# Making the high and low activation parts of two expert slots in one operation each

## The reference

```python
u = jnp.take(expert_u, eidx, axis=0)
a = jnp.einsum('thkd,td->thk', u, hc).astype(jnp.float32)
act = (jax.nn.gelu(a, approximate=False) * g).astype(hc.dtype)
vv = jnp.take(expert_v, eidx, axis=0)
return jnp.einsum('thk,thkd->td', act, vv)
```

## Time and profile before

| what | value |
|---|---|
| runs | 1316.86, 1319.37, 1319.6 us (median 1319.37) |
| profiled execution | 1320.85 us, of which 1318.7 us span |
| TensorE (PE) busy | 1304.0 us, 99% of the span |
| PE weight loads (PEld) busy | 1258.2 us, 95% |
| VectorE (DVE) busy | 1015.2 us, 77% |
| ScalarE (ACT) busy | 827.2 us, 63% |
| GpSimd (POOL) busy | 525.0 us, 40% |
| granted TensorE clock, mean | 0.997 of full speed |
| second expert layer | 674 to 1001 us of the span |

### The profile page before, as it was taken

The page is one execution under the profiler, slowest core; times in us unless marked ns, Lnnn a source line. Parts: engine busy times, 40 slices in busy tenths (PEclk is TensorE's granted clock), DMA queues, the critical chain, the costliest instruction groups (busy, mean ns, idle before and its releaser), DMA issues.

```text
span 1318.7 us, 24814 instructions
## 1 busy us (share of the span) xinstructions
PE 1304.0 (99%) x9818; PEld 1258.2 (95%) x9818; DVE 1015.2 (77%) x1845; ACT 827.2 (63%) x1679; POOL 525.0 (40%) x252
## 2 busy tenths in 40 slices
PE   9999999999999999999999999999999999999998
PEld 8999899999999999999999899999999999999997
DVE  4483645859999888899978798998867845899943
ACT  5564646545456888888865565555566666666653
POOL 3745567678901000000024444424205463794442
PEclk9999999999999999999999999999999999999999
DMA  8434345555656555555479999998865544556552
GB/s 301 139 111 128 118 139 177 165 175 177 196 189 200 199 168 167 162 174 162 164 249 332 353 332 328 327 343 316 310 212 169 171 133 130 188 166 196 186 191 97
DMA packets 74298, 268.35 MB, mean 203 GB/s; under 512 B 8252, under 2 KB 8636, under 8 KB 74184
## 3 DMA queue, kind: packets, MB, share of 16 engines
q1 hardware_dynamic: 64392, 232.17, 52.9%
q0 software_dynamic: 9216, 33.56, 6.9%
q10 hardware_dynamic: 576, 1.05, 0.2%
HBM read 265.70 MB, written 1.05 MB: 202 GB/s over the span
## 4 chain that ended last, share of the span: by engine, by line
PE 86%; DVE 10%; ACT 1%; DMA 1%; issue 0%; POOL 0%; SPq 0%; DVEq 0%; ACTq 0%
PE PS L611 85%; DMA RAW<-in_ev 1%; ACT SPL L1096 1%; DVE HS L1578 1%; DVE ixu L1839 1%; DVE Ssc L1833 1%; DVE ixu L1830 1%; PE PS L754 1%; DVE SPL L1549 1%; DVE bias L1628 0%; DVE top L1836 0%; DVE top L1827 0%; DVE HF L1566 0%; DVE qpc L1879 0%; DVE abu L1895 0%
## 5 line engine op out<-in xcount | busy, mean ns | idle before, releaser
L1096 ACT ACTIVATE SPL<-RAW 128x1024 fp32r<-128x1024 f32 x429 | 453.7, 1059 | 366.1 <-PE PS L611 350.7
L611 PE MATMUL PS<-HS,SPL 128*128 128x224 f32 (+2 forms) x3968 | 531.2, 292 | 1.1 <-DVE SPL L1549 0.9
L611 PEld LDWEIGHTS PS<-HS,SPL 128*128 128x128 f32 x3968 | 502.4, 189 | 12.7 <-issue 1.7
L2268 POOL TENSOR_TENSOR SPL<-RAW,SPL 128x1024 fp32r<-128x1024 f32 x149 | 361.7, 2432 | 261.1 <-ACT SPL L1096 261.1
L1549 DVE TENSOR_TENSOR SPL<-RAW,SPL 128x1024 fp32r<-128x1024 f32 x280 | 345.1, 1234 | 143.5 <-ACT SPL L1096 141.2
L611 PE MATMUL PS<-asp,SPL 128*128 128x448 f32 (+1 forms) x2048 | 321.9, 319 | 3.2 <-DVE SPL L1549 1.9
L611 PEld LDWEIGHTS PS<-asp,SPL 128*128 128x128 f32 x2048 | 307.5, 190 | 17.2 <-DVE SPL L1549 2.1
L2298 POOL DMA_INDIRECT rows<-in_er,RS x16 | 28.2, 1763 | 278.3 <-PE PS L611 247.7
L611 PE MATMUL PS<-HXb,SPL 128*128 128x256 f32 x720 | 89.3, 284 | 0.8 <-issue 0.6
L611 PEld LDWEIGHTS PS<-HXb,SPL 128*128 128x128 f32 x720 | 87.4, 188 | 1.4 <-issue 1.1
L1312 ACT ACTIVATE oh<-oh,T3f 128x128 f32<-128x128 f32 x224 | 71.4, 404 | 0.0
(11 more groups left out here) (296 smaller groups left out, 1529.5 us busy)
## 6 DMA issues: line engine op xcount, KB each, us to landing
RAW<-in_dense SPq DMA_DIRECT2D x176, 512.0 KB
RAW<-in_eu SPq DMA_DIRECT2D x128, 512.0 KB
RAW<-in_ev SPq DMA_DIRECT2D x128, 512.0 KB
bias<-in_nab SPq DMA_DIRECT2D x2, 768.0 KB, 6.9
XT<-in_xT ACTq DMA_DIRECT2D x4, 256.0 KB, 7.1
out_y<-HF SPq DMA_DIRECT2D x4, 256.0 KB, 2.2
c<-in_c SPq DMA_DIRECT2D x1, 960.0 KB, 9.0
c<-in_c SPq DMA_DIRECT2D x1, 512.0 KB, 4.7
```

The costliest lines, as they stand in the source:

```text
L611: return e.matmul(out, l, r, start=start, stop=stop, skip_group_check=skip)
L1096: e.activation(spl(n)[0], raw(n), ACT.Copy).then_inc(*up("act_high", ("hi", n)))
L2268: e.tensor_tensor(lo, raw(n), hi.bitcast(f32), ALU.subtract).then_inc(*up("pool_low", ("lo", n)))
```

## The change

The "a" steps 4 to 127 become 62 steps "a2", each for two neighbouring slots. Step "a2" of activations i and i + 1 stands before v step j = i - 2, for even j from 2 to 124. ScalarE writes both high parts in one operation (448 values per partition, into two regions of `asp`), after waiting for TensorE to be done with slot i - 3. VectorE makes both low parts in one operation, and both keys "apart" are given by that one. Activations 0 to 3 are made one by one as before. A region of the pair i, i + 1 was last used by slots i - 4 and i - 3.

```diff
@@ peer_steps
     for j in range(NE):
-        while ahead < min(j + 4, NE):
-            yield "a", ahead
-            ahead += 1
+        if j % 2 == 0 and 2 <= j < NE - 2:
+            yield "a2", ahead
+            ahead += 2
         if j == NE // 2:
             yield "late", 0
         yield "v", j
@@ build
         asp = [asp_[:, 4 + 512 * i:516 + 512 * i] for i in range(4)]
+        asp_pairs = asp_[:, 4:2052].rearrange("p (s c) -> p s c", s=4)
@@ act_program
+                elif what == "a2":
+                    w.wait_ge(*at("ev", "u", i + 1))
+                    w.wait_ge(*at("v", i - 3))
+                    e.activation(asp_pairs[:, i % 4:i % 4 + 2, 0:W], GB[:, i:i + 2, :], ACT.Copy).then_inc(
+                        *up("act_part", ("ahi", i), ("ahi", i + 1)))
@@ dve_program
+                elif what == "a2":
+                    w.wait_ge(*at("ahi", i))
+                    s = asp_pairs[:, i % 4:i % 4 + 2, :]
+                    e.tensor_tensor(s[:, :, W:2 * W], GB[:, i:i + 2, :], s[:, :, 0:W].bitcast(f32), ALU.subtract).then_inc(
+                        *up("dve_part", ("apart", i), ("apart", i + 1)))
```

## The result

The changed kernel takes 1322.26 us (median of 20 runs, 1319.07 to 1325.94), the kernel before 1319.32 us (20 runs). The ratio is 1.0026, with a 95% interval of 1.0017 to 1.0035: 3.4 us, between 2.2 and 4.6 (the two medians lie 2.9 us apart; the ratio is worked out over all the runs). The forecast was no change, 1319.4 us. The profiled execution of the changed kernel took 1324.95 us, 2.7 us above the median of its runs, so its rows show more than the mean loss.

The account below looks back on a forecast made before the run. TensorE was taken to bound the kernel, hiding the relief on VectorE and ScalarE; late pairs cost 0.05 us: 1320.85 + 0.05 = 1320.9 us profiled, 1319.4 for the runs, range 1316.0 to 1322.0.

Parts of the forecast that it names:

- It stays, within 0.2 us either way: Second expert layer, slot 32: TensorE's 1.9 us stall for a late weight transfer was to remain, within 0.2 us.
- T: Moment at which ScalarE starts the split of slot j + 2, after TensorE has finished slot j - 1.
- 0.54 us in hand in a usual step: Step 19, behind a long operation on VectorE: the pair ends at T + 4.06, 0.54 us in time.
- none at one crowded step: Step 65, with the angles' work besides: the pair would end at T + 4.60, just on the limit.
- the reserve of 4.60 us from T: Deadline for a pair on VectorE: done by T + 4.60 us, or TensorE waits.
- pairs come late: Rival: a pair over 1.16 us on VectorE delays TensorE at 34 steps; at 1.3 us, 4.8 us, 1324; chance 0.07.
- loads come late: Rival: shifted low parts start loads up to 0.23 us later; five late transfers cost 9.5 us, 1329; chance 0.03.
- the 9 us forecast: VectorE's busy time was to fall some 9 us by durations (62 x 0.156).
- The tie at the pair 68, 69: Crowded stretch, around 849 us: pair ends on its limit, T + 4.60; 0.16 us late if it takes 774 ns.
- The start's stall of 1.3 us: Start of the second expert layer: TensorE's 1.3 us wait was to stay, since activations 0 to 3 are untouched.
- VectorE's relief: Pairs save 4 us on VectorE, hidden by TensorE's work; gain on the path 0.
- the pairs' gain in waits on TensorE: Rival: TensorE waits 62 times less at slots' borders, 6.5 us would go, giving 1313; chance 0.04.

Follow-up runs that it names:

- e11: Changed kernel, all 62 pairs kept, with VectorE doing a step's long operation after the next step's pair instead of ahead of it; ratio 1.0001.
- e4: Changed kernel with two of the four extra loads ahead of slot 32 (c2, 960 KB, and poolw, 256 KB) moved to slot 112; ratio 0.9992.
- e2: Kernel before, with activations 32 and 33 alone made together before step 30, all others one by one; ratio 1.0015.
- e1: Changed kernel with one of its 62 pairs taken apart: activations 32 and 33 made one by one before steps 29 and 30; ratio 1.0012.
- e9: Changed kernel with five pairs around the late slot (activations 28 to 37) made one by one, the other 57 left; ratio 1.0011.
- e5: Kernel before, without pairs, with the loads c2 and poolw moved from ahead of slot 32 to slot 112; ratio 0.9991.

## Why the prediction was wrong

**The step that failed** is "It stays, within 0.2 us either way", of the stall at slot 32. I worked out when a pair must be done from T, ScalarE's start after TensorE's release, and found 0.54 us in hand in a usual step and none at one crowded step. But in that one stall ScalarE starts by the transfer, nearly 5 us after TensorE's release, and the reserve of 4.60 us from T means nothing there. The pair stands behind the slot's low part and a long operation, so its delay adds to the slot's in full: 1.82 us, and the stall grew from 1.87 to 4.10 us. I had both rows in hand, the late transfer and the pair's new place in the queue, and worked out each alone. The late slot should have been run through the new order: low part, 1.20 us, 0.62 us, TensorE.

**The rival that came true** is "pairs come late", by its mechanism and not by its price or its point. It was to need an operation of over 1.16 us; it took 620 ns. It was to cost at 34 steps; the main cost is at one. It had a chance of 0.07. Its neighbour "loads come late" looked at late transfers, but the slot came only 0.3 us later: it's the work between its arrival and TensorE that grew.

**A term I left out** is the clock. I read 1.00 in every stretch of the layer and took a stall to cost its own length. About half of the loss, 1.75 of 3.6 us by the means, is clock.

**What stays open** is where the whole of the mean loss lies. That the pair 32, 33 behind the late slot lengthens the stall is shown by the timelines, of e11 above all; that the loss as a whole hangs on VectorE's order and on the late loads is shown by e11 (1.0001) and e4 (0.9992), each with all 62 pairs. That this one pair makes all of the loss is not: e2 has about half of it, and e1 and e9, without it, keep 1.0012 and 1.0011.

**What held.** VectorE's pair was put at 618 ns and took 620, ScalarE's at 566 and took 563; VectorE's time on the low parts fell from 48.8 us to 38.5 and two single ones, the 9 us forecast. The tie at the pair 68, 69 was put at 0 to 0.16 us: in the profile after, the pair starts at 852.92 for T = 848.83, T + 4.09, its end releases TensorE after 0.14 us (as in the chain above at 760.32) and not 0.05, and the weight loads pause for 0.19 us (the third wait above, for "issue", is elsewhere: it is at the last slots).

```profile
848.83 1.06 ACT L1097 ACTIVATE SPL<-RAW 128x1024 fp32r<-128x1024 f32 x1 [1.44 <-PE PS L612]
...
852.92 0.62 DVE L2076 TENSOR_TENSOR asp<-GB,asp 128x448 fp32r<-128x448 f32 x1
...
853.65 3.45 PEld L612 LDWEIGHTS PS<-asp,SPL 128*128 128x128 f32 x22 [0.19 <-issue]
```

The start's stall of 1.3 us stayed. That TensorE bounds the layer and that VectorE's relief is worth nothing held too: with the late loads gone, pairs or none are one time. And the pairs' gain in waits on TensorE, a rival at 1313 us, did not come: e4 is no faster than e5.

## What to carry to other kernels

When operations are put together or moved in a queue, take the latest thing that stands ahead of them in each queue, not the steady step: find the transfer that is late today and run it through the new order. Two operations made one are needed when the first was, and are done behind all that the second used to stand behind. And price a stall by what the clock does after it, which can be as much again; where one burst of loads makes the stall, try moving the burst first.

## What the runs showed that I had not expected

The granted clock was at 0.50 for 5.94 us after a stall of 4.10 us, and in the profiles with stalls from 2.94 to 3.49 us it cost 1.65 us each. And the same slot behind the same loads reached ScalarE from 2.54 us before TensorE ran out of work to 0.61 us behind it. The runs of one kernel differ by several us; this and the fall of the clock at 120 to 140 us may be a part of it, but each kernel was profiled only once.
